# Packing the input tiles of a three-branch attention mixer, and moving the sample queries' selection behind branch B

## The chip, the cores and the metric

The kernel runs on one NeuronCore of a Trainium2 chip. The metric is the time of one execution in microseconds, the median of several runs. The core has TensorE (PE in the profile, its weight loads PEld), VectorE (DVE), ScalarE (ACT), GpSimd (POOL) and SyncE (SP), each with its own instruction stream; they wait for each other by semaphores.

## What is computed

Two layers of a streaming encoder, over 512 prompt tokens and 32 sample tokens (which also see 256 cached ones). Each layer is a half-step FFN, a mixer, and a second half-step FFN. Only the mixer changes:

```python
u = rmsnorm(x, P['mix_pre_gain'][l])
(q_lat, kv_lat, k_r, q_b, k_b, v_b, q_c, k_c, v_c, q_i, k_i, w_i,
 g_a, g_b, g_c) = jnp.split(u @ P['w_in'][l], IN_OFFSETS, axis=-1)
...
# A: latent attention with a rotary key of 32, k_rope = rope(k_r, q_pos)
# B: stick-breaking attention, 8 heads of 64
# C: sparse attention: scores from the indexer, top-k keys, then softmax over those
rel = relu(einsum('bqhd,bkd->bqhk', q_i, k_i) * D_IDX ** -0.5)
score = einsum('bqhk,bqh->bqk', rel, w_i * H_IDX ** -0.5)
_, sel = lax.top_k(score, kk)      # kk = 128 for the prompt, 72 for the sample
...
merged = (sigmoid(g_a) * (o_a @ w_br[0]) + sigmoid(g_b) * (o_b @ w_br[1]) + sigmoid(g_c) * (o_c @ w_br[2]))
x = x + rmsnorm(merged @ w_o, P['mix_post_gain'][l])
```

The widths in u @ w_in: index keys (ki) 64, C's keys (kc) 64, C's values (vc) 64, rotary key (kr) 32, index weights (wi) 8, index queries 512, C's queries 512, latents 384 and 256, B's queries, keys and values 512 each.

## The kernel before

All activations are held feature-major, 128 features on the partitions by 544 tokens. A product of u with 128 columns of weights is a "tile". To keep fp32 accuracy with one-pass matmuls both factors are split into a high and a low part: for each tile ScalarE copies the weights' high half to `piece_m` (`high`, L1118), GpSimd subtracts it in the ring of weights (`low`, L424), and TensorE does 3 x 8 x 2 matmuls of 272 columns (`split_product`, L621 with the high half and L626 with the low one). Products of small factors (`product`, L582) are plain fp32.

The tiles of a mixer have a fixed order, `TILES`. Two PSUM units of two banks each take turns: tile t goes to unit t % 2. TensorE opens a tile when the one before it on the same unit has been evacuated (`vacated`), and the evacuating engine waits for `done`. The order and who evacuates:

- kI (index keys, twice, so that both halves of the partitions hold them), qI0-3, kC (C's keys, twice), vw (C's values and index weights), all by ScalarE, which first makes the high half of the weights two tiles on (`evac`) and then copies. kI and qI0 are computed together (`first_pair`), since u arrives piece by piece. `to_keys` (L1199 to L1201) evacuates with three copies: prompt tokens in two parts, sample tokens.
- v0, v1 (B's values, tokens on the partitions, L734), in four weight pieces that each feed five token blocks; the vw tile is transposed between them.
- The indexer loop: 16 steps of an index score pair (L754), with qC0-3 cut into spans of 12 matmuls between them (L828). VectorE sums the scores over the heads (L1553).
- kr and krs: the rotary key and its half-swapped copy, each four times over on the partitions; then ql0-2, kv0-1, qB0-3, kB0-3. Column sums of squares (L596, two fp32 matmuls of 272 columns against ones) are put between some of them.
- Branch B (L876 to L928) on TensorE, ScalarE and VectorE in a chain, with one round of the top-k search for query block 3 after each of VectorE's steps.
- uq0-3 (evacuated by ScalarE), qr0, qs0, qr1, qs1 (by VectorE, which multiplies with the rotary factors, L1588), kA0-3, vA0-3 (ScalarE). Then attention A and C with the merges (L859) in between, and the output projection wo0-7.

VectorE's order in a mixer: index sums, `select(1)`, `select(2)`, `rotate_keys` (L1662 to L1666), the norms of the latents, `select(4)` (the sample queries: 9 MAX8 and 8 MATCH_REPLACE8 over 288 scores at L1632 and L1634, and eight closing instructions at L1647 to L1654), branch B, `select_last(3)` (the same eight closing instructions over 512 scores), then qr0. GpSimd also issues the DMAs for caches and output rows (`row`), and after branch B splits its output (L498, L500). SyncE loads the weights into a ring of four slots, `MIX_CHUNKS`: the chunk k + 4 is asked for when the last tile that uses chunk k is done.

Of the kernel before, what the change touches and what calls it, by code (L numbers as in the profile page):

```python
# [34 lines left out]
P = 128  # L35
DEPTH, D, D_FF = 2, 1024, 2816
SEQ, NEW, PAST = 512, 32, 256
TOK = SEQ + NEW
# [32 lines left out]
PC_MIX = 30 + 48 + 8  # L71
# [56 lines left out]
IN_PIECES = ([(i // 2, (i % 2) * 1024, 1024) for i in range(6)]  # L128
             + [(3, 0, 1024)] + [(4 + i // 2, (i % 2) * 1024, 1024) for i in range(4)]
             + [(6 + i // 2, (i % 2) * 1024, 1024) for i in range(19)])  # L130
# [3 lines left out]
PIECE_OF = {t: i for i, t in enumerate(TILES[:7])} | {t: 11 + i for i, t in enumerate(TILES[9:28])} | {f"wo{n}": 78 + n for n in range(KD)}  # L134
# [3 lines left out]
def build(nc, d):  # L138

    with ExitStack() as ctx:  # L140
# [15 lines left out]
        cst = sb("cst", [P, 6, P])  # L156
# [61 lines left out]
        kr_raw = region(22296, 2, TOK)  # L218
# [109 lines left out]
        def _(sp):  # L328
# [78 lines left out]
        def _(pool):  # L407
# [27 lines left out]
            for l in range(DEPTH):  # L435
# [33 lines left out]
                evacuated("kI")  # L469
                row("p_ki", kI[0:DH, 0:SEQ], "rows_ki")  # L470
                row("s_ki", kI[0:DH, KEY_NEW:NKEY], "rows_ki")
                lows(4, 13)
                evacuated("v0")
                evacuated("v1")
                evacuated("kC")
# [6 lines left out]
                lows(13, 30)  # L482
# [19 lines left out]
                def gate_low(m):  # L502
                    low(l, PC_M, 30 + 2 * m, (CH_M + 20 + m, 0), 0, 1024)

                def branch_low(m):
                    low(l, PC_M, 31 + 2 * m, (CH_M + 20 + m, 1), 1024, 512)
# [32 lines left out]
                for n, (ch, at, m) in enumerate(OUT_PIECES):  # L539
                    low(l, PC_M, 78 + n, (CH_M + ch, n % 2), at, m)  # L540
# [6 lines left out]
        def _(pe):  # L547
# [144 lines left out]
            def mixer(l):  # L692
# [10 lines left out]
                def split_tile(name, x_h, x_l, chunk_of, at):  # L703
                    t, piece = TILE[name], PIECE_OF[name]
                    open_tile(l, t % 2, T_M + t // 2)
                    split_product(l, t % 2, l * PC_LAYER + PC_M + piece, piece % 2, ring_r[:, (ch + chunk_of) % NSLOT, at:at + 1024],
# [6 lines left out]
                for i in range(2, 7):  # L713
# [11 lines left out]
                for i in range(4):  # L725
                    piece = 7 + i
# [22 lines left out]
                for p in range(16):  # L749
# [6 lines left out]
                    tile_span(l, f"qC{p // 4}", u_h, u_lo, IN_PIECES[11 + p // 4], 12 * (p % 4), 12 * (p % 4) + 12)  # L756
# [12 lines left out]
                for i in range(8):  # L769
                    w = chunk(l, ch + 16 + i // 4)  # L770
                    at = (i % 4) * KQ * P
                    tile(TILES[28 + i], [(w[:, at + k * P:at + k * P + P], ql[:, k, :]) for k in range(KQ)])
# [60 lines left out]
            def merge_span(l, m, u, a, e):  # L833

                b = MERGES[m][0]
                piece = l * PC_LAYER + PC_M + 30 + 2 * m
# [241 lines left out]
        def _(act):  # L1078
# [92 lines left out]
            def mixer(l):  # L1171
                def high_in(i):
                    if i < 30:
                        ch, at, n = IN_PIECES[i]
                        high(CH_M + ch, 0, i % 2, at, n, l)
                    elif 78 <= i < 78 + KD:
                        ch, at, n = OUT_PIECES[i - 78]
                        high(CH_M + ch, 0, i % 2, at, n, l)
# [28 lines left out]
                to_keys("kI", kI)  # L1207
# [14 lines left out]
                high_in(9)  # L1222
# [3 lines left out]
                A(wI[:, 0:4, :], vw[:, :, DH:DH + H], ACT.Copy)  # L1226
                A(VC[:, 6, :], PS[:, 6, 0:DH], ACT.Copy)
                A(wI[:, 4, :], PS[:, 6, DH:DH + H], ACT.Copy)
                for i in range(1, 3):
                    act.wait_ge(S["v_step"], l * 3 + i + 1)  # L1230
                    high_in(9 + i)
                for n in range(2):
                    u = evac(f"v{n}")
                    if n:
                        high_in(12)
# [183 lines left out]
        def _(dve):  # L1419
# [118 lines left out]
            def mixer(l):  # L1538
# [234 lines left out]
def shape_constants():  # L1773
# [3 lines left out]
    cst = np.zeros((P, 6, P), np.float32)  # L1777
# [5 lines left out]
    cst[:, 5] = np.where((k < CHUNK) & (q >= CHUNK), -BIG, 0)  # L1783
    pos = np.concatenate([np.arange(SEQ), PAST + np.arange(NEW)]).astype(np.float32)
# [116 lines left out]
```

## Time and profile before

| | |
|---|---|
| runs, median | 3258.82 us (3257.35 to 3259.65, 3 runs) |
| profiled execution | 3259.87 us |
| its span, first to last instruction | 3258.1 us |
| granted clock of TensorE, mean | 0.982 of 2.4 GHz |
| PE busy | 3078.2 us (94%) |
| PEld busy | 2855.6 us (88%) |
| DVE busy | 1546.2 us (47%) |
| ACT busy | 958.5 us (29%) |
| POOL busy | 1067.7 us (33%) |
| DMA | 255.48 MB, mean 78 GB/s |

### The profile page before, as it was taken

Reading aid. Unit: us, or ns where it says so; the run is one execution under the profiler, and the core shown is the slowest. Engines: PE = TensorE matmul, PEld = TensorE weight load, DVE = VectorE, ACT = ScalarE, POOL = GpSimd, SP = SyncE. Lnnn points to the kernel's source line nnn. Section 1 sums busy time; section 2 is a strip of 40 time slices with the busy share of each in tenths; the row PEclk is TensorE's granted clock in tenths of the full one; section 3 lists DMA queues with packets and bytes.
Section 4 is the critical chain, followed back from the end, with each engine's and each line's share of the span. In section 5 each row is a group of like instructions: output and inputs, shape, how many; then the busy total and the mean of one; then the engine's idle time right before and its main releaser. Section 6 shows DMA issues by size and latency. Waiting matters only on the chain. (4 is left out here: it accounts for less than half of the span.)

```text
span 3258.1 us, 54238 instructions
## 1 busy us (share of the span) xinstructions
PE 3078.2 (94%) x22974; PEld 2855.6 (88%) x22974; DVE 1546.2 (47%) x1857; ACT 958.5 (29%) x1519; POOL 1067.7 (33%) x499
## 2 busy tenths in 40 slices
PE   8999979999999989999899999799999899899997
PEld 7999977956878979999899999679578789899997
DVE  4554242862355446553265532338533554555523
ACT  3222233362333232222232222332623332322221
POOL 3434323312222323343333433333022324244332
PEclk9999989999999999999999999899999999999998
DMA  6221232112111222222212212312021113222221
GB/s 177 86 82 67 88 122 82 69 45 66 41 54 55 89 93 78 90 82 72 105 65 90 86 63 97 123 69 80 21 75 40 62 41 104 85 81 90 78 81 63
DMA packets 43103, 255.48 MB, mean 78 GB/s; under 512 B 6048, under 2 KB 6144, under 8 KB 26048
## 3 DMA queue, kind: packets, MB, share of 16 engines
q1 hardware_dynamic: 37008, 235.64, 20.3%
q0 software_dynamic: 5840, 17.50, 2.0%
q8 instruction: 117, 1.92, 0.2%
q14 instruction: 42, 0.34, 0.0%
q10 hardware_dynamic: 96, 0.08, 0.0%
HBM read 237.34 MB, written 15.85 MB: 78 GB/s over the span
## 5 line engine op out<-in xcount | busy, mean ns | idle before, releaser
L424 POOL TENSOR_TENSOR ring_r<-ring,piece_h 128x1024 fp32r<-128x1024 f32 (+1 forms) x240 | 630.7, 2630 | 1019.3 <-ACT piece_h L1118 1019.3
L424 POOL TENSOR_TENSOR ring_r<-ring,piece_m 128x1024 fp32r<-128x1024 f32 (+1 forms) x172 | 366.5, 2135 | 909.9 <-ACT piece_m L1118 909.7
L1118 ACT ACTIVATE piece_h<-ring 128x1024 fp32r<-128x1024 f32 (+1 forms) x240 | 274.7, 1146 | 1147.4 <-PE PS L626 1138.6
L621 PE MATMUL PS<-uT_r,piece_h 128*128 128x272 f32 x2688 | 555.1, 288 | 6.1 <-DVE sq L1520 6.1
L621 PE MATMUL PS<-u_l,piece_h 128*128 128x272 f32 x2688 | 554.9, 288 | 0.0
L626 PE MATMUL PS<-uT_r,ring_r 128*128 128x272 f32 x3328 | 449.9, 287 | 0.0
L626 PEld LDWEIGHTS PS<-uT_r,ring_r 128*128 128x128 f32 x3328 | 429.6, 188 | 0.0
L621 PEld LDWEIGHTS PS<-uT_r,piece_h 128*128 128x128 f32 x2688 | 421.8, 188 | 7.0 <-ACT piece_h L1118 7.0
L621 PEld LDWEIGHTS PS<-u_l,piece_h 128*128 128x128 f32 x2688 | 419.4, 188 | 0.0
L621 PE MATMUL PS<-act_l,piece_h 128*128 128x272 f32 x1408 | 292.1, 289 | 0.0
L621 PE MATMUL PS<-act_h,piece_h 128*128 128x272 f32 x1408 | 291.5, 288 | 0.0
L1473 DVE TENSOR_TENSOR rstd<-rstd,sq 128x544 f32<-128x544 f32 x36 | 106.7, 2964 | 359.0 <-ACT sq L1090 359.0
L1118 ACT ACTIVATE piece_m<-ring 128x1024 fp32r<-128x1024 f32 (+1 forms) x172 | 160.6, 936 | 340.0 <-PE PS L626 220.0
L1522 DVE TENSOR_TENSOR sq<-sq,rstd 128x544 f32<-128x544 f32 x88 | 219.2, 2491 | 83.8 <-ACT sq L1137 83.8
L621 PEld LDWEIGHTS PS<-act_l,piece_h 128*128 128x128 f32 x1408 | 220.7, 188 | 0.0
L621 PEld LDWEIGHTS PS<-act_h,piece_h 128*128 128x128 f32 x1408 | 220.5, 189 | 0.0
L1530 DVE TENSOR_TENSOR act_l<-sq,act_h 128x544 f32 x88 | 214.0, 2432 | 10.8
L626 PE MATMUL PS<-act_h,ring_r 128*128 128x272 f32 x1408 | 186.5, 287 | 0.0
L626 PEld LDWEIGHTS PS<-act_h,ring_r 128*128 128x128 f32 x1408 | 180.5, 188 | 0.0
L859 PE MATMUL PS<-uT_r,piece_m 128*128 128x272 f32 x768 | 166.6, 299 | 1.9 <-DVE xT L1613 1.9
L859 PE MATMUL PS<-u_lm,piece_m 128*128 128x272 f32 x768 | 161.3, 292 | 0.0
L1527 DVE TENSOR_TENSOR act_h<-sq,PS 128x544 f32 x88 | 63.5, 721 | 168.9 <-PE PS L626 168.3
(248 smaller groups left out, 4715.0 us busy)
## 6 DMA issues: line engine op xcount, KB each, us to landing
ring<-in_w_up SPq DMA_DIRECT2D x88, 1024.0 KB, 4.7
ring<-in_w_dn SPq DMA_DIRECT2D x64, 704.0 KB, 4.1
ring<-in_w_mg SPq DMA_DIRECT2D x48, 768.0 KB, 4.4
ring<-in_w_in SPq DMA_DIRECT2D x24, 1024.0 KB, 4.8
ring<-in_w_out SPq DMA_DIRECT2D x8, 1024.0 KB, 4.8
x_spill<-xT SPq DMA_DIRECT2D x2, 2176.0 KB, 8.9
xT<-x_spill SPq DMA_DIRECT2D x2, 2176.0 KB, 9.1
ring<-in_w_vb SPq DMA_DIRECT2D x4, 1024.0 KB, 4.8
```

The source lines that it names most:

```text
L424: nc.gpsimd.tensor_tensor(ring_r[:, ch[0] % NSLOT, at:at + n], w, hi, ALU.subtract).then_inc(S["w_low"], 1)
L621: mm(PS[:, 2 * u + b, 0:HALF], w, x[k][:, HALF * b:HALF * b + HALF], start=first and k == 0 and n == 0, stop=False)
L626: ins = mm(PS[:, 2 * u + b, 0:HALF], w_l[:, k * P:(k + 1) * P], x_h[k][:, HALF * b:HALF * b + HALF], start=False, stop=last and k == K - 1)
L859: ins = mm(PS[:, 2 * u + j % 2, 0:HALF], w, x[:, k, half], start=j < 2, stop=j >= 6 * K - 2)
L1118: A(buf[:, hs, 0:n], ring[:, ch % NSLOT, at:at + n], ACT.Copy).then_inc(S["w_high"], 1)
L1473: ins = V.tensor_tensor(rstd[:], rstd[:], sq[:, k % 2, :], ALU.add) if k else V.tensor_copy(rstd[:], sq[:, 0, :])
L1522: V.tensor_tensor(g, g, rstd[:], ALU.mult).then_inc(S["gate_step"], 1)
L1527: V.tensor_tensor(halves(hi), halves(g), up, ALU.mult).then_inc(S["gate_step"], 1)
L1530: V.tensor_tensor(lo, g, hi.bitcast(F32), ALU.subtract).then_inc(vacated[1], 1)
```

## The change

The columns of w_in are packed anew. The first tile, "kk", holds the index keys in rows 0 to 63 and C's keys in rows 64 to 127; ScalarE copies each of them to both halves of its destination, in 12 copies of 64 partitions. The tile vw now holds C's values (rows 0 to 63), the rotary key (64 to 95) and the index weights (96 to 103). The tiles kr and krs stay as PSUM tiles, but are made from vw's rows 64 to 95 by a 0/1 matrix in the constants, one plain product of 32 rows each. So the mixer has 27 weight pieces instead of 30, and an empty tile "pad" keeps the count of tiles even. B's value weights come in four chunks of 1024. VectorE does `select(4)` after branch B, behind `select_last(3)`.

```diff
-PC_MIX = 30 + 48 + 8
+N_IN = 27
+PC_MIX = N_IN + 48 + 8
...
-    t = ["kI"] + [f"qI{i}" for i in range(4)] + ["kC", "vw", "v0", "v1"]
+    t = ["kk"] + [f"qI{i}" for i in range(4)] + ["vw", "v0", "v1"]
     t += [f"qC{i}" for i in range(4)] + ["kr", "krs"] + [f"ql{i}" for i in range(KQ)] + [f"kv{i}" for i in range(KKV)]
...
-    t += [f"kA{i}" for i in range(4)] + [f"vA{i}" for i in range(4)]
+    t += [f"kA{i}" for i in range(4)] + [f"vA{i}" for i in range(4)] + ["pad"]
...
+V_CHUNKS = 4
+LATE_TILES = TILES[8:12] + TILES[14:27]
 MIX_CHUNKS = ([("w_in", i, 2048, TILES[2 * i + 1]) for i in range(3)]
-              + [("w_vw", 0, 1024, "vw"), ("w_vb", 0, 2048, "v1"), ("w_vb", 1, 2048, "v1")]
-              + [("w_in", 3 + i, 2048 if i < 9 else 1024, TILES[min(10 + 2 * i, 27)]) for i in range(10)]
+              + [("w_vb", i, 1024, f"V{i}" if i + 1 < V_CHUNKS else "v1") for i in range(V_CHUNKS)]
+              + [("w_in", 3 + i, 2048 if i < 8 else 1024, LATE_TILES[min(2 * i + 1, 16)]) for i in range(9)]
...
-        cst = sb("cst", [P, 6, P])
+        cst = sb("cst", [P, 8, P])
...
-                    if by in TILE:
+                    if by in V_DONE:
+                        sp.wait_ge(S["v_step"], l * 3 + V_DONE[by])
+                    elif by in TILE:
                         consumed(l, TILE[by] % 2, turn_of(by))
...
-                for i in range(2, 7):
+                for i in range(2, 6):
                     split_tile(TILES[i], u_h, u_lo, IN_PIECES[i][0], IN_PIECES[i][1])
...
-                for i in range(15, 30):
-                    name = TILES[9 + i - 11]
-                    split_tile(name, u_h, u_lo, IN_PIECES[i][0], IN_PIECES[i][1])
+                for i, name in enumerate(("kr", "krs")):
+                    tile(name, [(cst[64:96, 6 + i, :], vw_f[64:96, 0:TOK])])
+                for name in LATE_TILES[4:]:
+                    split_tile(name, u_h, u_lo, *IN_PIECES[PIECE_OF[name]][:2])
...
                 for name in ("vA2", "vA3"):
                     pe.wait_ge(vacated[TILE[name] % 2], l * T_LAYER + turn_of(name) + 3)
+                alone(pe)
+                pe.sem_inc(done[TILE["pad"] % 2], 1)
+                pe.sem_inc(vacated[TILE["pad"] % 2], 1)
...
-                to_keys("kI", kI)
+                u = evac("kk")
+                for r, dst in ((0, kI), (DH, kC)):
+                    for e in range(2):
+                        to = dst[DH * e:DH * e + DH]
+                        A(to[:, 0:HALF], PS[r:r + DH, 2 * u, 0:HALF], ACT.Copy)
+                        A(to[:, HALF:SEQ], PS[r:r + DH, 2 * u + 1, 0:SEQ - HALF], ACT.Copy)
+                        ins = A(to[:, KEY_NEW:NKEY], PS[r:r + DH, 2 * u + 1, SEQ - HALF:HALF], ACT.Copy)
+                ins.then_inc(vacated[u], 1)
...
-                to_keys("kC", kC)
                 to_blocks("vw", vw_f)
...
-                select(l, 4, 3)
                 dve.wait_ge(S["rows_ki"], 16 * (l * 2 + 2))
                 branch_b(l)
-                select_last(l, 3, 4)
+                select_last(l, 3, 3)
+                select(l, 4, 4)
                 dve.wait_ge(S["rows_out"], 16 * (l * 12 + 12))
...
+    m = np.arange(P)
+    cst[64 + m % ROPE, 6, m] = 1
+    cst[64 + (m + ROPE // 2) % ROPE, 7, m] = 1
...
-    cols = np.concatenate([part["ki"], part["ki"], part["qi"], part["kc"], part["kc"], part["qc"],
-                           part["kr"], part["kr"], part["kr"], part["kr"], krs, krs, krs, krs, part["ql"], part["kv"],
-                           part["qb"], part["kb"], part["kv"][:128]])
+    none = np.full(P, at[-1])
+    cols = np.concatenate([part["ki"], part["kc"], part["qi"], part["vc"], part["kr"], part["wi"], none[:24],
+                           part["qc"], part["ql"], part["kv"], part["qb"], part["kb"], none])
```

## Rows read from the trace of the kernel before

**Rows 1.** The page's head.
```profile
span 3258.1 us, 54238 instructions
```

**Rows 2.** Windows: length, busy us (instructions) of PE, PEld, DVE, ACT, POOL, clock, DMA, GB/s.
```profile
573.90:669.00 95.10, 94.76 (x741) 93.74 (x739) 75.26 (x161) 27.31 (x48) 36.47 (x18) 1.00 0.23 80
739.95:790.00 50.05, 49.36 (x204) 32.16 (x205) 14.16 (x14) 9.85 (x14) 7.08 (x2) 0.97 0.15 48
```

**Rows 3.** Timeline of ACT, first layer: start, us, engine, line, operation [idle before <- releaser].
```profile
467.35 0.38 ACT L1199 ACTIVATE arena<-PS 128x272 f32<-128x272 f32 x1
...
467.96 1.07 ACT L1118 ACTIVATE piece_m<-ring 128x1024 fp32r<-128x1024 f32 x1
...
573.99 1.06 ACT L1118 ACTIVATE piece_m<-ring 128x1024 fp32r<-128x1024 f32 x1 [0.99 <-PE PS L828]
574.96 0.61 ACT L1205 ACTIVATE arena<-PS 128x544 f32<-128x544 f32 x1
...
580.00 1.06 ACT L1118 ACTIVATE piece_m<-ring 128x1024 fp32r<-128x1024 f32 x1 [4.44 <-PE PS L626]
...
598.01 1.06 ACT L1118 ACTIVATE piece_m<-ring 128x1024 fp32r<-128x1024 f32 x1 [3.92 <-PE PS L626]
...
604.95 1.06 ACT L1118 ACTIVATE piece_m<-ring 128x1024 fp32r<-128x1024 f32 x1 [4.85 <-PE PS L626]
```

**Rows 4.** Timeline of PE, first layer.
```profile
468.13 0.52 PE L621 MATMUL PS<-uT_r,piece_m 128*128 128x272 f32 x2 [1.53 <-ACT arena L1201]
...
500.50 0.47 PE L734 MATMUL PS<-piece_m,uT_r 128*128 128x512 f32 x1 [2.06 <-ACT arena L1214]
...
739.95 4.68 PE L582 MATMUL PS<-arena,ring 128*128 128x272 f32 x12 [0.68 <-ACT arena L1345]
...
746.91 30.26 PE L582 MATMUL PS<-arena,ring 128*128 128x272 f32 x116
```

**Rows 5.** Window of the first weights' arrival, columns as in rows 2.
```profile
12.00:14.00 2.00, 0.00 (x0) 0.00 (x0) 0.00 (x0) 0.98 (x2) 1.07 (x1) 1.00 0.98 410
```

**Rows 6.** Timeline of DVE, first layer.
```profile
648.27 0.45 DVE L1632 MAX8 m<-xT 128x8 f32<-128x288 f32 x1
...
658.34 2.05 DVE L1647 TENSOR_SCALAR xT<-xT,m 128x288 f32<-128x288 f32 x1
...
661.31 0.37 DVE L1650 TENSOR_SCALAR xT<-xT,m 128x288 f32<-128x288 f32 x1
...
664.33 0.55 DVE L1673 MEMSET arena<- 128x256 f32 x2 [0.19 <-DVE arena L1654]
...
672.07 0.42 DVE L1680 SCALAR_TENSOR_TENSOR arena<-PS,sq 128x256 f32<-128x256 f32 x1 [7.19 <-ACT sq L1338]
...
750.07 5.62 DVE L1651 TENSOR_TENSOR_SCAN xT<-xT 128x512 f32<-128x512 f32 x1
...
758.28 0.72 DVE L1588 TENSOR_TENSOR arena<-PS,ropes 128x544 f32<-128x544 f32 x1 [0.39 <-PE PS L582]
...
760.96 0.72 DVE L1588 TENSOR_TENSOR arena<-PS,ropes 128x544 f32<-128x544 f32 x1 [1.96 <-PE PS L582]
```

**Rows 7.** Timeline of DVE, second layer.
```profile
2370.84 0.73 DVE L1588 TENSOR_TENSOR arena<-PS,ropes 128x544 f32<-128x544 f32 x1 [0.40 <-PE PS L582]
```

**Rows 8.** Timeline of POOL, first layer.
```profile
657.82 2.40 POOL L424 TENSOR_TENSOR ring_r<-ring,piece_m 128x1024 fp32r<-128x1024 f32 x1 [3.61 <-ACT piece_m L1118]
...
749.76 4.85 POOL L500 TENSOR_TENSOR o_l<-arena,o_h 128x2176 fp32r<-128x2176 f32 x1
```

**Rows 9.** Windows of 1 us, columns as in rows 2.
```profile
501.00:502.00 1.00, 1.00 (x4) 0.76 (x3) 0.00 (x0) 0.00 (x0) 0.98 (x1) 0.57 1.00 426
532.00:533.00 1.00, 0.00 (x0) 0.00 (x0) 0.00 (x0) 0.99 (x2) 1.00 (x1) 1.00 0.84 319
2765.00:2766.00 1.00, 1.00 (x7) 1.00 (x6) 0.00 (x0) 0.00 (x0) 0.00 (x0) 0.50 1.01 244
```

**Rows 10.** The chain that ended last, in order of time: start, us, what.
```profile
2764.47 5.65 PE PS L621 x32
```

More of the change, by code:

```diff
@@ L126 @@
 assert len(MIX_CHUNKS) == CH_MIX
-IN_PIECES = ([(i // 2, (i % 2) * 1024, 1024) for i in range(6)]
-             + [(3, 0, 1024)] + [(4 + i // 2, (i % 2) * 1024, 1024) for i in range(4)]
-             + [(6 + i // 2, (i % 2) * 1024, 1024) for i in range(19)])
+IN_PIECES = ([(i // 2, (i % 2) * 1024, 1024) for i in range(6)] + [(3 + i, 0, 1024) for i in range(V_CHUNKS)]
+             + [(7 + i // 2, (i % 2) * 1024, 1024) for i in range(17)])
+assert len(IN_PIECES) == N_IN
 OUT_PIECES = [(44 + i // 2, (i % 2) * 1024, 1024) for i in range(KD)]
-PIECE_OF = {t: i for i, t in enumerate(TILES[:7])} | {t: 11 + i for i, t in enumerate(TILES[9:28])} | {f"wo{n}": 78 + n for n in range(KD)}
+PIECE_OF = {t: i for i, t in enumerate(TILES[:6])} | {t: 10 + i for i, t in enumerate(LATE_TILES)} | {f"wo{n}": N_IN + 48 + n for n in range(KD)}
+V_DONE = {f"V{i}": i + 1 for i in range(V_CHUNKS - 1)}
 VA_KEYS = [(0, 1), (2, 3), (4, 5), (6,)]
@@ L468, in _ @@
                 lows(2, 4)
-                evacuated("kI")
+                evacuated("kk")
                 row("p_ki", kI[0:DH, 0:SEQ], "rows_ki")
                 row("s_ki", kI[0:DH, KEY_NEW:NKEY], "rows_ki")
-                lows(4, 13)
+                lows(4, 12)
                 evacuated("v0")
                 evacuated("v1")
-                evacuated("kC")
                 row("p_kc", kC[0:DH, 0:SEQ])
@@ L502, in gate_low @@
                 def gate_low(m):
-                    low(l, PC_M, 30 + 2 * m, (CH_M + 20 + m, 0), 0, 1024)
+                    low(l, PC_M, N_IN + 2 * m, (CH_M + 20 + m, 0), 0, 1024)
                 def branch_low(m):
-                    low(l, PC_M, 31 + 2 * m, (CH_M + 20 + m, 1), 1024, 512)
+                    low(l, PC_M, N_IN + 1 + 2 * m, (CH_M + 20 + m, 1), 1024, 512)
                 pool.wait_ge(S["sb_out"], l * 5 + 5)
@@ L539, in _ @@
                 for n, (ch, at, m) in enumerate(OUT_PIECES):
-                    low(l, PC_M, 78 + n, (CH_M + ch, n % 2), at, m)
+                    low(l, PC_M, N_IN + 48 + n, (CH_M + ch, n % 2), at, m)
                 ffn(l, PC_B, CH_B)
@@ L705, in split_tile @@
                     open_tile(l, t % 2, T_M + t // 2)
-                    split_product(l, t % 2, l * PC_LAYER + PC_M + piece, piece % 2, ring_r[:, (ch + chunk_of) % NSLOT, at:at + 1024],
+                    split_product(l, t % 2, l * PC_LAYER + PC_M + piece, (piece if piece < N_IN else piece - N_IN) % 2, ring_r[:, (ch + chunk_of) % NSLOT, at:at + 1024],
                                   x_h, x_l)
@@ L725, in mixer @@
                 for i in range(4):
-                    piece = 7 + i
+                    piece = 6 + i
                     slot, at, _ = IN_PIECES[piece]
@@ L771, in mixer @@
                     at = (i % 4) * KQ * P
-                    tile(TILES[28 + i], [(w[:, at + k * P:at + k * P + P], ql[:, k, :]) for k in range(KQ)])
+                    tile(TILES[27 + i], [(w[:, at + k * P:at + k * P + P], ql[:, k, :]) for k in range(KQ)])
                     if i == 0:
@@ L835, in merge_span @@
                 b = MERGES[m][0]
-                piece = l * PC_LAYER + PC_M + 30 + 2 * m
+                piece = l * PC_LAYER + PC_M + N_IN + 2 * m
                 w_l = ring_r[:, (CH_M + 20 + m) % NSLOT, :]
@@ L1172, in high_in @@
                 def high_in(i):
-                    if i < 30:
+                    if i < N_IN:
                         ch, at, n = IN_PIECES[i]
                         high(CH_M + ch, 0, i % 2, at, n, l)
-                    elif 78 <= i < 78 + KD:
-                        ch, at, n = OUT_PIECES[i - 78]
-                        high(CH_M + ch, 0, i % 2, at, n, l)
+                    elif N_IN + 48 <= i < N_IN + 48 + KD:
+                        ch, at, n = OUT_PIECES[i - N_IN - 48]
+                        high(CH_M + ch, 0, (i - N_IN) % 2, at, n, l)
                 high_in(0)
@@ L1805 @@
     swap = np.concatenate([np.arange(16, 32), np.arange(16)])
-    krs = part["kr"][swap]
-    cols = np.concatenate([part["ki"], part["ki"], part["qi"], part["kc"], part["kc"], part["qc"],
-                           part["kr"], part["kr"], part["kr"], part["kr"], krs, krs, krs, krs, part["ql"], part["kv"],
-                           part["qb"], part["kb"], part["kv"][:128]])
+    none = np.full(P, at[-1])
+    cols = np.concatenate([part["ki"], part["kc"], part["qi"], part["vc"], part["kr"], part["wi"], none[:24],
+                           part["qc"], part["ql"], part["kv"], part["qb"], part["kb"], none])
     w_in = a["w_in"].reshape(L, KD, P, -1)
+    w_in = np.concatenate([w_in, np.zeros((L, KD, P, 1), np.float32)], axis=3)
     def tiles(w, n):
@@ L1853 @@
         "w_dn": a["w_ffn_down"].reshape(L, 2, 2, 11, P, KD, P).transpose(0, 1, 5, 2, 4, 3, 6).reshape(L, 32, P, 1408),
-        "w_in": groups(tiles(w_in[..., cols], 26), 2),
-        "w_vb": w_in[..., part["vb"]].reshape(L, 2, 4, P, 512).transpose(0, 1, 3, 2, 4).reshape(L, 2, P, 2048),
-        "w_vw": tiles(np.concatenate([w_in[..., vcwi], np.zeros((L, KD, P, P - len(vcwi)), np.float32)], axis=3), 1),
+        "w_in": groups(tiles(w_in[..., cols], 24), 2),
+        "w_vb": w_in[..., part["vb"]].reshape(L, 4, 2, P, 512).transpose(0, 1, 3, 2, 4).reshape(L, 4, P, 1024),
         "w_uq": groups(tiles(uq[..., uq_cols], 8), 4),
```

19 lines of the change are left out of this document (9 added, 10 removed).

## Prediction

> **What bounds the kernel now.** I read the page first, then the stages of the mixer as windows, then the timelines of ScalarE, TensorE, VectorE and GpSimd through one mixer, and last the same places in the second layer. The span is 3258.1 us [rows 1]. The stretch from the last piece of the indexer loop to branch B has TensorE busy for 94.76 of 95.10 us, and the stretch behind branch B for 49.36 of 50.05 us [rows 2]. So in both stretches that the change touches, TensorE sets the pace: an instruction taken from it shortens the kernel by its whole length, and anything that makes it wait lengthens the kernel by the whole wait. The question is how much of either there is, and how much slack VectorE has in each of the two.
>
> **What is removed.** One split tile (a 128-wide output tile of u @ w_in, 48 matmuls of 272 columns) takes 6.0 us: ScalarE starts the high half of the next weights when each tile is done, at 573.99 and then at 580.00 [rows 3]. Three such tiles go from each mixer: the tile of C's keys ahead of the value pieces, and the rotary key and its swapped copy behind the indexer loop. That is 3 x 6.0 = 18.0 us per layer, all of it TensorE's. Their three weight passes on ScalarE and GpSimd go too, beside TensorE, and their DMA is not waited for; they count nothing. Likewise nothing: the value weights in four chunks of 1024 instead of two of 2048 (one chunk is still asked for some three pieces before it is used), the padded vw tile (same 128 columns), and the new order of slots.
>
> **What is added, term by term, per layer.**
> - The packed first tile: nine more copies. Before, its three copies took from 467.35 to 467.96, 0.61 us, and TensorE waited 1.53 us for the last of them before the third tile could open [rows 3, 4]. Now there are four sets of three, each on 64 partitions. If a copy costs by its columns, the extra is 3 x 0.61 = 1.8 us, all in that wait; if half the partitions cost half, the four sets are worth two of the old, and the extra is 0.6 us. Nothing in the trace is cheaper for fewer partitions, so I take 1.8 and keep 0.6 for the range. The rule on ScalarE is the same: the Trainium skill (ScalarE: Activation LUTs, section What ACT_TABLE_LOAD costs) counts an ACTIVATE by elements per lane, 186 ns + 0.833 ns each, with some 93 ns of overlap between neighbours. By it a set would be 0.73 us and the extra 2.2; the row has 0.61, and the sum goes by the row.
> - Rotary key and its swap, now selected from the packed tile by a matrix of ones: 2 fp32 matmuls of 272 columns each. The same pair is seen where a column sum of squares is put between two tiles: 604.95 - 598.01 = 6.94 us instead of 6.01, so 0.93 us a pair [rows 3]. The second must wait for the unit of qC3: its weight pass and copy take from 573.99 to about 575.58 (574.96 + 0.61), 1.6 us. So 1.6 + 0.93 = about 2.6 us until the next tile starts, with 1.9 (both products, no wait) and 3.5 (ScalarE's copy of the first is waited for too) as bounds.
> - The empty tile "pad": one nop and two increments on TensorE, 0.1 us, at most 0.3.
> - Constants of 8 instead of 6 planes: 131 KB more in a start where the queues move 410 GB/s and ScalarE waits for weights [rows 5]: 0.3 us, once; none at the least, 0.6 at the most.
>
> **What is moved.** The selection for the sample queries, select(4), leaves its place before branch B and follows select_last(3) behind it. It issues no DMA. In its old place it ran from 648.27 to 664.33, and VectorE's first job of branch B then still waited 7.19 us for ScalarE [rows 6]: it was hidden, and taking it away frees nothing. It also was no obstacle for the shorter stretch: TensorE now starts branch B 9.4 us earlier after the indexer loop (12.0 - 2.6), and without select(4) VectorE is free at 648.3, over 11 us before that. Had it stayed, its end with the two MEMSETs at 664.9 would have been at most 2 us behind that first job (672.07 - 9.4 = 662.7). Branch B itself is unchanged.
>
> In the new place VectorE has almost no slack. It finished select_last(3) at 757.89, because it had waited only 0.39 us for the product of qr0 when it started on it at 758.28 [rows 6]; in the second layer that wait is 0.40 [rows 7]. Now it first does select(4). Length: 664.33 - 648.27 = 16.06 us as shown, but in it the comparison of L1647 took 2.05 us while GpSimd's weight pass ran from 657.82 to 660.22, and the like comparison at 661.31 took 0.37 [rows 6, 8]. In the new place GpSimd has finished its split (749.76 + 4.85 = 754.6) and waits for weights until attention [rows 8], so I take 16.06 - 1.68 = 14.4 us and keep 16.1 as the upper bound. The Trainium skill gives the reason (GPSIMD Engine Reference, section Specifications: GpSimd shares its SBUF interfaces with VectorE, and the two contend when VectorE reads through both ports); by that rule the lower value holds, and the trace agrees, 2.05 against 0.37 us.
>
> Who waits: qr0 and qs0 are evacuated by VectorE, and the next tile on qr0's unit is qr1. VectorE reaches qr0 at 757.9 + 14.4 = 772.3 and frees it at 773.1 (0.72 us, and a step to signal). TensorE has finished qs0 at 760.9, where VectorE's wait of 1.96 us for it ends [rows 6]. It stands still 773.1 - 760.9 = 12.2, with the signal 12.3 us; bounds 11.5 and 14.0. Behind it in TensorE's queue are qr1, qs1, the eight kA and vA tiles and all of attention, 30.26 us of unbroken matmuls from 746.91 for a start [rows 4]; nothing there waits for something that was not delayed as well, so the stall is not given back.
>
> Then the clock. After the gap before the output projection TensorE ran at the lower of its two levels, 1.2 GHz (granted 0.50 at 2765), and 32 matmuls took 5.65 us instead of the 4.0 that are their share of a 6.0 us tile [rows 9, 10]. In the first layer 12 matmul records behind branch B took 4.68 us, against some 2.7 for such a tile in the run that follows [rows 4]. A stall of 12 us ends the same way: 1.8 us, between 1.6 and 2.2.
>
> Sum per layer: -18.0 + 1.8 + 2.6 + 0.1 + 12.3 + 1.8 = +0.6 us. Twice that, and 0.3 at the start, is +1.5.
>
> One more term is open. The gap before the third tile grows from 1.5 to 3.4 us. A gap of 2.06 us ahead of the value pieces was followed by the lower level (0.57 in the window at 501), while a longer one behind them, in which the window at 532 lies whole, went by at 1.00 [rows 4, 9]. By the price above a fall costs 1.6 us. I count it in one of the two layers, +1.6, with none and both as bounds.
>
> Result: 1.5 + 1.6 = +3.1 us. Made against the profiled execution, 3259.87 us (its span of 3258.1 and 1.8 around it), that is 3263.0; from the median of the runs, 3258.82, it is **3262 us**. Changes under 0.2%, 6.5 us, can't be told from none here.
>
> **The rivals.**
> - *The stall at qr1 is not there, or is mostly absorbed* (faster). Then the 12.3 and the 1.8 go: 3262 - 28.2 = 3233.8 us in full, 3248 with half of it. It decides by VectorE's slack at qr0, which would have to be over 14 us; both layers show 0.4. For it speaks only that a time saved ahead of branch B is certain, while a stall is worked out. Chance 0.13.
> - *The added waits are all at their upper bound* through one cause, ScalarE and the clock: the 3.4 us gap drops the clock in both layers (+1.6), the copy of kr is waited for too (2 x 0.9 us), and the fall after the stall takes 2.2 (2 x 0.4): 3262 + 4.2 = 3266 us; with select(4) still slowed to 16.1 us, 3269.6. It passes the bound to slower from 3265.3. For it: the clock fell after a shorter gap. Against: GpSimd is idle there. Chance 0.26.
> - *The change does not do what it says*: the stretch before branch B does not shorten, because VectorE's chain of selections, not TensorE, starts it. Then 9.4 us of the gain are lost in each layer: 3281 us. Against it are the 7.19 us of slack and the 14 us that VectorE no longer has to do there. Chance 0.03.
> - The forecast, within 3252.3 to 3265.3: 0.58.
>
> **How the numbers follow.** Faster by over 0.2%: the first rival, 0.13. Slower: the second and third, 0.29. The same: 0.58. Bounds of the forecast: all low ends, 2 x (-18.0 + 0.6 + 1.9 + 11.5 + 1.6) = -4.8, give 3254; all high ends give 3270. The range reaches a little into the first rival, to 3251, and ends at 3270; outside it are most of the first rival and the third.
>
> **What would show each step.** In the new trace: per layer 3 x 48 fewer matmuls of the split product before branch B, and 4 fp32 ones with 32 rows; the third tile's wait near 3.4 us; from the indexer loop's end to branch B 85.7 instead of 95.1 us; VectorE at MAX8 of 288 columns directly behind L1654's last step after branch B; a wait of TensorE for VectorE before qr1 of about 12 us, in both layers, with a lower granted clock behind it; the stretch behind branch B near 64 us instead of 50. The prediction is wrong if that wait is under 6 us or over 16, or if the stretches before branch B shorten by other than 13 to 14 us per layer.

## The result, and the profile after

The changed kernel takes **3275.5 us**, the median of five runs (3269.5 to 3277.45), against 3257.6 us for the kernel before in the same comparison. The ratio is 1.0047, with a 95% interval of 1.0033 to 1.0062: slower, by about 18 us. The prediction was 3262 us with a range to 3270, so the time lies outside it, on the slow side. The profiled execution of the changed kernel is one of its fastest, 3269.5 us with a span of 3267.7 us.

The page's head and its row for TensorE:

```profile
span 3267.7 us, 53682 instructions
...
PE 3056.2 (94%) x22702; PEld 2829.2 (87%) x22702; DVE 1537.5 (47%) x1857; ACT 955.5 (29%) x1525; POOL 1051.9 (32%) x493
```

There are 272 matmuls fewer: 288 of the six split tiles are gone, 16 of the four kr and krs products have come. The removal took place, and yet the span grew by 9.6 us. The waits of TensorE, as total us, times, longest one:

```profile
PE PS L587 <- DVE arena L1603: 24.6, 2, 12.3
...
PE PS L626 <- ACT arena L1222: 7.5, 2, 3.7
```

The first is new: the stall ahead of qr1, once in each layer. The second was 3.1 us in all before, 1.53 at the longest. VectorE's timeline shows where it comes from [rows 6 has the same engine before]:

```profile
744.38 0.43 DVE L1669 TENSOR_SCALAR arena<-xT 128x512 bf16<-128x512 f32 x1
744.91 0.46 DVE L1647 MAX8 m<-xT 128x8 f32<-128x288 f32 x1
...
754.99 0.37 DVE L1662 TENSOR_SCALAR xT<-xT,m 128x288 f32<-128x288 f32 x1
...
758.82 0.31 DVE L1669 TENSOR_SCALAR arena<-xT 128x288 bf16<-128x288 f32 x1
759.30 1.36 DVE L1603 TENSOR_TENSOR arena<-PS,ropes 128x544 f32<-128x544 f32 x2 [0.17 <-DVE arena L1669]
```

`select(4)`, the rows on 288 columns, starts at 744.91 right behind `select_last(3)` and ends at 759.13, 14.2 us later; its comparison takes 0.37 us here, not the 2.05 of [rows 6]. Only then are qr0 and qs0 taken out of PSUM, in one go, for both had long been done. TensorE's timeline of the places where the change adds or moves a wait:

```profile
470.32 0.82 PE L626 MATMUL PS<-uT_r,piece_m 128*128 128x272 f32 x2 [3.75 <-ACT arena L1222]
...
498.17 0.47 PE L739 MATMUL PS<-piece_m,uT_r 128*128 128x512 f32 x1 [2.06 <-ACT arena L1230]
...
529.64 0.70 PE L759 MATMUL PS<-arena 64*128 64x256 f32 x4 [3.00 <-ACT arena L1252]
...
569.97 1.18 PE L587 MATMUL PS<-arena,cst 32*128 32x272 f32 x4
571.70 1.27 PE L587 MATMUL PS<-arena,cst 32*128 32x272 f32 x4 [0.55 <-ACT arena L1214]
572.90 0.82 PE L626 MATMUL PS<-uT_r,piece_m 128*128 128x272 f32 x2
...
760.17 6.16 PE L587 MATMUL PS<-arena,ring 128*128 128x272 f32 x18 [12.31 <-DVE arena L1603]
```

And the stretches of [rows 2] as windows (the first now begins with kr and krs, the second with uq0; the third is the second one's like in the second layer), with two short windows inside the first (columns as in rows 2):

```profile
569.97:658.17 88.20, 86.77 (x654) 84.72 (x653) 59.45 (x128) 25.81 (x48) 31.16 (x16) 0.98 0.22 74
728.57:791.64 63.07, 49.70 (x204) 32.25 (x205) 25.77 (x47) 10.21 (x14) 7.08 (x2) 0.89 0.12 39
2345.80:2412.17 66.37, 53.03 (x204) 34.39 (x205) 25.77 (x47) 10.18 (x14) 7.09 (x2) 0.86 0.11 37
...
573.00:576.00 3.00, 3.00 (x13) 3.00 (x14) 2.38 (x9) 0.62 (x1) 0.57 (x1) 0.50 0.38 161
...
578.00:581.00 3.00, 3.00 (x26) 3.00 (x25) 2.17 (x9) 0.36 (x1) 0.00 (x0) 1.00 0.01 3
```

The last two are the same kind of work, split products of 272 columns, with TensorE never idle: 13 matmuls in 3 us at a granted clock of 0.50 (1.2 GHz), 26 at 1.00 (2.4 GHz). What is done at the lower level takes twice as long. Such short stretches turn out to be the subject of this case.

I put one number on them for each kernel, the **low-clock work**: over windows of 1 us from 400 us to the end, the busy time of TensorE times twice what the granted clock lacks to 1.00, added up. It is the time for which TensorE worked at the lower level, and half of it is what the level cost. The kernel before has 61.7 us of it, the changed one 80.9. Half of the difference is 9.6 us, and the spans differ by 9.6 us. So by this count all of the slowdown of this pair of executions is clock, and the rest of the change, stall included, adds up to zero. Experiments 7, 9 and 11 test it.

### The profile page after: what moved, and what is told of

Same layout as the page of the kernel before. It is cut to its first block and busy times, and to the rows that moved or that the text cites. A ratio compares the mean times of both kernels' runs of the same rounds, so it can differ in the third digit from the quotient of the medians.

```text
span 3267.7 us, 53682 instructions
## 1 busy us (share of the span) xinstructions
PE 3056.2 (94%) x22702; PEld 2829.2 (87%) x22702; DVE 1537.5 (47%) x1857; ACT 955.5 (29%) x1525; POOL 1051.9 (32%) x493
## 5 line engine op out<-in xcount | busy, mean ns | idle before, releaser
L430 POOL TENSOR_TENSOR ring_r<-ring,piece_m 128x1024 fp32r<-128x1024 f32 (+1 forms) x166 | 350.9, 2118 | 933.5 <-ACT piece_m L1127 933.3
L631 PE MATMUL PS<-uT_r,ring_r 128*128 128x272 f32 x3232 | 436.8, 287 | 0.0
L631 PEld LDWEIGHTS PS<-uT_r,ring_r 128*128 128x128 f32 x3232 | 417.2, 188 | 0.0
```

The source lines that it names most:

```text
L430: nc.gpsimd.tensor_tensor(ring_r[:, ch[0] % NSLOT, at:at + n], w, hi, ALU.subtract).then_inc(S["w_low"], 1)
L631: ins = mm(PS[:, 2 * u + b, 0:HALF], w_l[:, k * P:(k + 1) * P], x_h[k][:, HALF * b:HALF * b + HALF], start=False, stop=last and k == K - 1)
```

## The experiments

All kernels are the changed one (or the one before, where it says so) with the edit shown. The first four ran beside the kernel before on one chip (3259.04 us there), the next four on one (3259.16), the last four on one (3259.20). All results in one table:

| kernel | median us | ratio to before, 95% interval | profiled span | low-clock work | span less half of it |
|---|---|---|---|---|---|
| before | 3257.6 | | 3258.1 | 61.7 | 3227.3 |
| changed | 3275.5 | 1.0033 to 1.0062 | 3267.7 | 80.9 | 3227.3 |
| 1 select back | 3243.49 | 0.9937 to 0.9962 | 3241.8 | 78.7 | 3202.5 |
| 2 select behind qr | 3244.96 | 0.9943 to 0.9969 | 3242.6 | 80.7 | 3202.3 |
| 3 before, move alone | 3286.41 | 1.0070 to 1.0096 | 3284.6 | 65.7 | 3251.8 |
| 4 stall filled | 3269.78 | 1.0019 to 1.0037 | 3269.5 | 86.7 | 3226.2 |
| 5 = 2 + kk shared | 3228.54 | 0.9896 to 0.9926 | 3225.5 | 50.3 | 3200.4 |
| 6 = 2 + kr early | 3231.90 | 0.9902 to 0.9929 | 3232.7 | 67.3 | 3199.1 |
| 7 all gaps filled | 3252.33 | 0.9972 to 0.9990 | 3250.3 | 41.1 | 3229.8 |
| 8 = 2 + 5 + 6 | 3229.70 | 0.9893 to 0.9923 | 3227.9 | 64.4 | 3195.7 |
| 9 before, gaps filled | 3253.92 | 0.9980 to 0.9998 | 3251.7 | 46.6 | 3228.4 |
| 10 = 8, filled | 3229.42 | 0.9895 to 0.9923 | 3229.3 | 67.2 | 3195.7 |
| 11 = 1, filled | 3230.01 | 0.9896 to 0.9925 | 3229.0 | 50.6 | 3203.7 |
| changed, again | 3275.56 | 1.0030 to 1.0055 | 3273.7 | 92.1 | 3227.7 |

The last column is the kernel's time with the clock's share taken out. It falls into groups that follow the waits alone, as the experiments show one by one.

**The moved selection (1, 2, 3).** Number 1 puts `select(4)` back, number 2 puts it later still, number 3 does the move alone to the kernel before.

```diff
 # 1
+                select(l, 4, 3)
                 dve.wait_ge(S["rows_ki"], 16 * (l * 2 + 2))
                 branch_b(l)
-                select_last(l, 3, 3)
-                select(l, 4, 4)
+                select_last(l, 3, 4)
 # 2
                 select_last(l, 3, 3)
-                select(l, 4, 4)
...
                     dve.wait_ge(S["qr_ready"], l * 2 + g + 1)
+                select(l, 4, 4)
                 attend(l, 0)
```

> The changed kernel with select(4) put back ahead of branch B; all of the packing stays. Theory A (the move costs TensorE 12.3 us of waiting per layer ahead of qr1, and 2 to 3 us of lower clock behind it): about 2 x 15 = 30 us below the changed kernel's 3275, so 3245, and 12 us below the kernel before. Rival B (the packing is what costs, through its own gaps and the lower clock that they leave, and the move is mostly covered): less than 10 us below the changed kernel, 3265 or more. VectorE should reach branch B in time; if it is late, by 2 us per layer at most.

> The changed kernel with select(4) moved further back, behind the two rotary query tiles (qr, qs) and ahead of attention, where VectorE was seen idle for 23 us. Theory A: the wait ahead of qr1 is gone and 14.4 us fit into the idle time, so the same as with select(4) ahead of branch B, about 3245. Rival (VectorE's work anywhere behind branch B delays attention): the start of attention is late by 5 us or more per layer, 3255 or more.

> The kernel before with only select(4) moved behind select_last(3); nothing of the packing. Theory A: 12.3 us of waiting and 2 to 3 us of lower clock per layer more than before, 3258 + 29 = 3287. Rival B: under 10 us more, below 3268. If the two parts add up, the distance of this kernel from the one before and that of the changed kernel from the one with select(4) put back are alike within 4 us.

The move alone costs 27.4 us (3286.41 against 3259.04). Its waits show the two stalls and nothing else of that size:

```profile
PE PS L582 <- DVE arena L1588: 24.6, 2, 12.3
```

With the clock taken out, the move is worth 3251.8 - 3227.3 = 24.5 us, which is the wait. Undoing it in the changed kernel gives 3202.5, which is 24.8 lower. In the medians the two differ more: 27.4 us in the kernel before, 32.0 in the changed one (3275.5 and 3243.49), where alike within 4 us had been expected. The rest is the clock: half of the low-clock work is 2.0 us more with the move in the kernel before, and 6.7 more in the changed one by its repeated run (92.1 and 78.7). Behind the qr and qs tiles it costs nothing either, since VectorE is then waited for by no tile; TensorE's run through that place, in number 2, has no gap:

```profile
743.68 25.12 PE L587 MATMUL PS<-arena,ring 128*128 128x272 f32 x94
768.63 1.88 PE L794 MATMUL PS<-ring,arena 128*128 128x512 f32 x4
```

So without the move the change is a gain of some 15 us (0.4 to 0.6%), and the stall is of the size that was predicted.

**The clock behind the stall (4).** 25 products of no use for TensorE ahead of qr1, so that the wait stays but TensorE works in it.

```diff
+                    if i == 6:
+                        filler(25)
```

> The changed kernel with 25 fp32 matmuls of 272 columns of no use, 11.3 us, put on TensorE ahead of qr1, where it otherwise waits 12.3 us for VectorE; they write a free bank. Theory C (the low clock behind the wait costs 1.8 us in the first layer and 2.6 in the second): 4.4 us less than the changed kernel, near 3271, with the granted clock at 1.00 behind the wait. Rival (the wait alone is the cost, the clock behind it costs nothing): no difference within 1 us. If the filling delays qr1, it is up to 2 us more.

```profile
743.80 8.41 PE L587 MATMUL PS<-arena,ring 128*128 128x272 f32 x36
752.05 11.62 PE L724 MATMUL PS<-ropes,cst 128*128 128x272 f32 x50
764.44 1.87 PE L587 MATMUL PS<-arena,ring 128*128 128x272 f32 x7 [0.77 <-DVE arena L1610]
```

The window behind it, at 762 to 766, was granted 1.00 (0.52 in the changed kernel at 760 to 764, behind its stall), in both layers. The median fell by some 5.7 us, more than the 4.4 that the two stretches held. But the runs of number 4 go from 3256.15 to 3274.43 us, so that a step of this size says little by itself, and the profiled execution had 86.7 us of low-clock work, more than the changed kernel's 80.9: stretches that its first profile did not have stood at other gaps. One execution was not enough to tell which of them belong to the kernel.

**The changed kernel again.** For that reason the same kernel was run once more.

> The changed kernel once more, unchanged, to see which of its low-clock stretches a second profiled execution has. Theory 1 (the stretches differ between executions, as its times of 3269.5 to 3277.5 us do): a profile with another set of them, and a span that differs by half of the difference in work done at the low clock. Rival: the same stretches and the same span, 3267.7 us.

This execution, 3275.46 us, is the one at the median. Two windows of it beside the same two of the first profile, first the repeated run:

```profile
500.00:503.00 3.00, 2.80 (x7) 2.25 (x8) 0.00 (x0) 0.00 (x0) 1.67 (x1) 0.52 0.29 113
534.00:537.00 3.00, 3.00 (x14) 2.74 (x16) 0.84 (x2) 0.60 (x2) 2.99 (x6) 0.55 0.75 246
```

and the first profile of the changed kernel:

```profile
500.00:503.00 3.00, 3.00 (x15) 2.44 (x14) 0.00 (x0) 0.00 (x0) 0.00 (x0) 1.00 0.00 0
534.00:537.00 3.00, 3.00 (x23) 2.31 (x22) 1.17 (x3) 0.66 (x2) 0.00 (x0) 1.00 0.61 199
```

The waits ahead of both are the same to 0.01 us in the two executions, 2.06 and 3.00 us; one lost the clock behind them and the other did not. The low-clock work is 92.1 against 80.9 us, half of the difference is 5.6, and the spans differ by 6.0 us. Its six runs go from 3263.39 to 3277.74 us. Against the kernel before it is (92.1 - 61.7) / 2 = 15.2 us of 15.6.

**All gaps filled, in both kernels (7, 9).** If the clock is the whole loss, the two kernels must come out alike once TensorE is hardly still in these gaps. Number 7 also keeps the 25 products of number 4 ahead of qr1.

```diff
 # 7 (9: three ahead of the third tile, four, six)
+                filler(8)
                 for i in range(2, 6):
                     split_tile(TILES[i], u_h, u_lo, IN_PIECES[i][0], IN_PIECES[i][1])
...
+                filler(4)
                 banks = [2 * (TILE[f"v{s // 2}"] % 2) + s % 2 for s in range(4)] + [4]
...
+                filler(6)
                 pe.wait_ge(S["cache_in"], (l * N_CACHE + N_CACHE) * 16)
...
                 for i, name in enumerate(("kr", "krs")):
+                    if i:
+                        filler(1, 5)
```

> The changed kernel with additional products of no use in each of the gaps that it has on TensorE ahead of branch B and ahead of the qr tile (8 ahead of the third tile, 4 ahead of the v tiles, 6 behind them, 1 between kr and krs, 25 ahead of the rotated query), so that the waits stay and TensorE is never still in them. Theory 1 (the low-clock stretches are what is left of the loss): all stretches of both layers go, 10 to 17 us less than the changed kernel, 3258 to 3265 us. Rival (the stretches come anyway, at another place): no better than with the filling at the rotated query alone, 3268 to 3272 us.

> The kernel before with additional products of no use in its own three gaps (3 ahead of the third tile of the mixer's inputs, 4 ahead of the v tiles, 6 behind them), so that its waits stay and TensorE isn't still in them. Theory (a low-clock stretch follows each of these gaps and costs half of the work done in it): the stretches of before that lie there go, 5 to 10 us less, 3249 to 3254 us, so that the two kernels come out alike once their gaps are filled (3252 us with the change). Rival (the fillings helped the changed kernel for another reason): no change, 3259 us.

Filling took 23 us from the changed kernel, more than either theory had said, since I had worked from its first, fortunate profile; half of 92.1 - 41.1 would be 25.5. The kernel before gained 5.3 us; half of its 61.7 - 46.6 would be 7.6. The products themselves cost 1 to 2.5 us where they outlast the wait, as the table's last column shows (3229.8 and 3228.4 against 3227.3). Filled, the two stand at 3252.3 and 3253.9 us: the difference of 18 us is gone, although qr1 of number 7 still comes only when VectorE has freed its unit. The same windows behind the gap ahead of the v tiles, first of the kernel before and then of it with its gaps filled:

```profile
500.00:504.00 4.00, 3.50 (x10) 2.77 (x11) 0.00 (x0) 0.24 (x2) 1.98 (x1) 0.64 0.55 233
```
```profile
500.00:504.00 4.00, 3.77 (x17) 2.83 (x16) 0.00 (x0) 0.58 (x3) 2.31 (x1) 1.00 0.54 229
```

Numbers 9 and 7, in this order, also give the terms of the change at an even clock, first layer: from the pair of the first two tiles to the third tile 15.92 and 18.36 us, third tile to v 32.37 and 26.35, indexer loop's end to branch B 95.59 and 86.66, uq0 to attention 48.39 and 61.22.

**The select back, filled (11).** The fillings of number 7 in number 1.

> The changed kernel with the select moved back ahead of branch B and additional products in the gaps (8, 4, 6 and 1). Theory: the clock is that of the changed kernel with all gaps filled (3252 us), and the two stalls of 12.3 us are gone, 3228 us; against the filled kernel before (3249 to 3254 us) that is the worth of the packing without its waits' clock, 21 to 26 us. Rival: 3232 to 3240 us, the filling does less here.

3230.0 us, 23.9 below the filled kernel before: this is the worth of the packing with its stall and its clock taken away, 12 us a layer. The rival of 3232 to 3240 is excluded by the run's own spread (3229.15 to 3230.80).

**Shorter waits instead of fillings (5, 6, 8, 10).** Number 5 lets VectorE copy C's keys while ScalarE copies the index keys; number 6 puts the kr and krs products behind the v tiles, into the 3.00 us gap; number 8 does both, and number 10 fills what gaps it has left. All have the select where number 2 has it.

```diff
 # 5, ScalarE and VectorE
-                for r, dst in ((0, kI), (DH, kC)):
-                    for e in range(2):
+                for e in range(2):
+                    to = kI[DH * e:DH * e + DH]
+                    A(to[:, 0:HALF], PS[0:DH, 2 * u, 0:HALF], ACT.Copy)
...
+                for e in range(2):
+                    to = kC[DH * e:DH * e + DH]
+                    V.tensor_copy(to[:, 0:HALF], PS[DH:P, 0, 0:HALF])
...
+                ins.then_inc(S["kk_half"], 1)
 # 6, TensorE, moved up from behind the indexer's loop
+                for i, name in enumerate(("kr", "krs")):
+                    tile(name, [(cst[64:96, 6 + i, :], vw_f[64:96, 0:TOK])])
                 pe.wait_ge(S["cache_in"], (l * N_CACHE + N_CACHE) * 16)
```

> The select behind the qr and qs tiles, as in the second experiment (3245.0 us), and the sets of copies out of the kk tile shared: ScalarE copies the index keys, VectorE C's keys, so that a set should last about 0.37 us on ScalarE instead of 0.74 us, and the third tile of the mixer's inputs should wait about 2.2 us instead of 3.75 us. Theory 1 (only the waits count): 1.5 us less in each layer, 3242 us. Theory 2 (waits and the clock after them): where the shorter gap leaves the clock up, 1.7 us more for each layer, 3238.5 us. Rival: VectorE takes longer for its two copies out of PSUM than ScalarE saves, and the gap stays; 3245 us.

> The select behind the qr and qs tiles, and the kr and krs products of both layers moved ahead of the indexer's loop, right behind the v tiles, where TensorE stood still for 3.0 us. Theory 1 (only the waits count): the kr and krs products fill that gap and their own waits go, 1.4 us less in each layer, 3242 us. Theory 2 (with the clock): the low-clock stretch behind kr and krs (1.7 us a layer) goes too, and that behind the gap ahead of the indexer's loop, 3238.5 us. Rival: the copies of kr and krs on the other engines hold up the first score tiles of the indexer by as much; 3245 us.

> The select behind the qr and qs tiles, the copies out of the kk tile shared between ScalarE and VectorE, and the kr and krs products ahead of the indexer's loop, all three together. Theory 1 (waits alone add up): 3245 less 3 and 3, 3239 us. Theory 2 (with the clock): 3232 to 3236 us. Rival (low-clock stretches only move to other places): 3241 to 3245 us.

> The version with the select behind the qr and qs tiles, shared kk copies and early kr and krs, and additional products in its three gaps (4, 4 and 3). Its profile at 3230 us had 64 us of TensorE work in low-clock stretches, the changed kernel with all gaps filled 41. Theory: half of the difference goes, 12 us, 3218 us. Rival (stretches move to other places whatever is filled): 3227 to 3231 us.

In number 5 the third tile waits 2.29 us instead of 3.75:

```profile
470.15 0.48 PE L627 MATMUL PS<-uT_r,piece_m 128*128 128x272 f32 x2 [2.29 <-ACT arena L1223]
```

The kernel gained 16.4 us on number 2 by the medians, where 0 to 6.5 had been expected, and 17.1 by the profiled spans. Of these, 1.9 us stay with the clock taken out; the other 15.2 are the low-clock work, down from 80.7 to 50.3 us. The stretch behind the third tile, for one, is gone in this execution. First number 2, then number 5:

```profile
471.00:475.00 4.00, 3.04 (x15) 3.04 (x16) 0.00 (x0) 2.78 (x9) 2.41 (x2) 0.68 0.01 3
```
```profile
470.00:474.00 4.00, 3.85 (x31) 3.88 (x32) 0.00 (x0) 1.82 (x5) 3.93 (x3) 1.00 0.16 62
```

So is its like in the second layer. But those behind the v gap (499 to 504 in number 2), the indexer's gap (both layers) and branch B's end (second layer) are gone too, which number 5 did not touch: their waits are as long as ever. The one behind kr and krs stayed, in both layers; here is the first:

```profile
571.00:574.00 3.00, 3.00 (x14) 2.92 (x14) 2.48 (x8) 0.62 (x1) 0.85 (x1) 0.51 0.47 197
```

Number 6 also gained much more than its waits (13.1 us, 3.2 of them with the clock taken out). Number 8 has the shortest time of all with the clock taken out, 3195.7, as the two edits add up (1.9 + 3.2 = 5.1, and 6.6 came), and its median is below all that had been expected for it. But it has 64.4 us of low-clock work and so is no better than number 5. Filling its gaps (10) did nothing: 3229.42 us, the time that the rival named. Its mechanism is not what the traces show, though: the stretches did not move, all but one of them lie where number 8 has its own. Two of the three filled gaps, ahead of the third tile and of v, had no fall behind them in number 8, so there was nothing to win; behind the third, ahead of kr, the fall stayed in both layers. TensorE's timeline of number 10 at this third place, and the window behind it with the clock:

```profile
525.41 1.54 PE L712 MATMUL PS<-ropes,cst 128*128 128x272 f32 x6
526.87 1.18 PE L588 MATMUL PS<-arena,cst 32*128 32x272 f32 x4
528.37 1.18 PE L588 MATMUL PS<-arena,cst 32*128 32x272 f32 x4 [0.32 <-ACT arena L1261]
529.48 0.70 PE L771 MATMUL PS<-arena 64*128 64x256 f32 x4
```
```profile
531.00:534.00 3.00, 3.00 (x13) 2.10 (x12) 0.52 (x2) 0.16 (x1) 1.29 (x3) 0.50 1.00 365
```

TensorE was busy but for 0.32 us, and fell to the lower level all the same. Most of what ran just before were products on 32 and 64 rows; whether that is the reason was not tested. In number 11, where filling stands in this place and kr and krs don't, the window from 531 to 534 has a granted clock of 1.00.

Numbers 5, 8, 10 and 11 lie within 1.5 us of each other, all about 0.9% faster than the kernel before. Number 5 is the simplest that needs no useless products.

## Why the prediction was wrong

Its step "Then the clock", with the open term behind it, failed: it priced a fall of the clock about right and counted too few of them. It allowed for one fall of the clock behind each stall (1.8 us a layer) and one, in one of two layers, for the longer gap at the third tile (1.6 us): 5.2 us. The clock took 9.6 us in the first profile and 15.2 in the one at the median. The low-clock work of the two executions, first and second layer, at the three waits that the change adds or lengthens:

| behind | first profile | repeated run | half of it, both layers | predicted |
|---|---|---|---|---|
| third tile's wait, 3.75 us | 3.2, 3.3 | 3.3, 3.3 | 3.3 | 1.6 |
| kr and krs, with 0.55 us between | 3.4, 3.4 | 3.4, 3.4 | 3.4 | 0 |
| stall, 12.31 us | 3.6, 5.2 | 4.5, 5.2 | 4.4, 4.9 | 3.6 |

That is 11.1 and 11.6 us for the places of the change. The rest of the difference, -1.5 us in one execution and +3.6 in the other, lies at waits that both kernels have, as the v gap at 500, the indexer's at 534 and branch B's end. The stall of the second layer also cost more than its upper bound, 2.6 us against 2.2.

For the open term, the third tile's gap, one layer of two was too few. All six profiled executions in which that wait is 3.75 us (changed, changed again, 1, 2, 4, 6) have the fall in both layers; the four in which it is 1.53 or 2.3 us (before, 3, 5, 8) have it in neither. Behind kr and krs, with their 0.55 us between, the fall came in both layers of all six that have them there unfilled (changed, changed again, 1, 2, 4, 5). The other steps, per layer:

- **Stall at qr1**: predicted 12.3 us, measured 12.31. Length of `select(4)` in its new place: 14.4 predicted, 14.2 measured.
- **Three split tiles less**: predicted -18.0. The one ahead of the v tiles gave -6.02 (9 against 7). The other two and the kr and krs products gave -8.93 at an even clock, where -12.0 + 2.6 = -9.4 was predicted. In the changed kernel itself the stretch is 88.13 us where 85.7 was predicted, most of the difference being the low stretch at 572 to 576. From kr's start to the next tile it is 2.93 us, where 2.6 was predicted.
- **The stretches before branch B**: the prediction called itself wrong if they shortened by other than 13 to 14 us. From the first pair of tiles to branch B they shortened by 11.45 us in the first layer (452.35 to 669.54 before, 452.43 to 658.17 after) and 8.63 in the second (2066.55 to 2283.79, 2066.40 to 2275.01), by 12.4 in the filled pair, first layer. So by its own sign it was wrong here; the other, a wait ahead of qr1 under 6 or over 16 us, did not come.
- **Copies of the kk tile**: predicted +1.8, measured 3.75 - 1.53 = +2.2. A set of three copies of 64 partitions took 0.71 to 0.75 us from start to start, not the 0.61 of the old set. The estimate that the prediction worked out from the figures of the Trainium skill (ScalarE: Activation LUTs, section What ACT_TABLE_LOAD costs) was 0.73 and 2.2, and the trace agrees with it. The old set's 0.61 went from its first start to the start of the weight pass, which overlapped the last copy; to the end of that copy it is 0.73 as well. ScalarE's timeline, second set:

```profile
468.04 0.39 ACT L1220 ACTIVATE arena<-PS 64x272 f32<-64x272 f32 x1
468.34 0.35 ACT L1221 ACTIVATE arena<-PS 64x240 f32<-64x240 f32 x1
468.59 0.18 ACT L1222 ACTIVATE arena<-PS 64x32 f32<-64x32 f32 x1
468.78 0.39 ACT L1220 ACTIVATE arena<-PS 64x272 f32<-64x272 f32 x1
```

- **Sum without the clock**: predicted 2 x -1.2 + 0.3 = -2.1 us, measured 0.0 and +0.4 (last column of the table). This part of the forecast was low by 2.1 to 2.5 us in all, by terms that are each within half a microsecond a layer.

So of the 12.5 us by which the execution at the median lies above the forecast for a profiled one (3275.46 against 3263.0), 10.0 are falls of the clock that I had not counted, and 2.5 the other terms. In the first profile they are 4.4 and 2.1. What I had in hand would have warned me: the row at 501 showed a fall behind a gap of 2.06 us [rows 9], and the change adds or lengthens a wait at three places a layer. I counted the third tile's gap in one layer instead of both, and none behind kr and krs. My other row, the window at 532 at 1.00, lies inside its gap, and the falls seen here come behind a short gap; it could not have shown one. That the clock stayed up behind it too (1.00 at 533 to 538 before) was true of that execution and not of others. I had also read one execution as if its low stretches were the kernel's own. Of the rivals, the second had the right mechanism (3266 us, falls in both layers) and still had none behind kr and krs. It also had the copy of kr waited for; the gap there was 0.55 us. The first (no stall) and the third (no shorter stretch ahead of branch B) are excluded by the wait of 12.3 us and the stretch of 88.1 us.

What stays open is what decides whether a gap is followed by a fall. It isn't the length alone: 2.06 and 3.00 us did both in two executions of one kernel, and over all ten profiled executions with the v gap of 2.06 us unfilled, 8 of 20 were followed by a fall. Why shortening one wait by 1.5 us in number 5 also cleared stretches that lie at waits it did not touch was not separated from the shift of all later work that came with it.

## What to carry to other kernels

Before moving work to an engine with "free" time, find the first tile of another engine that it will stand ahead of there: `select(4)` cost nothing in its old place or behind the qr and qs tiles, and 25 us in between. Where TensorE is the bound, count every gap of a few microseconds twice, by its length and by the stretch at the lower clock that may follow it. Add up the low-clock work of more than one profiled execution before explaining a difference of half a per cent; with it taken out, spans compare to about a microsecond. And useless products in waits that can't be removed are cheap, but what they bring depends on whether a fall follows there: 23 us for the changed kernel, 5 for the one before, nothing for number 8.

## What the runs showed of the hardware

- Spans less half of the low-clock work agree within 0.4 us for the kernel before and two executions of the changed one (3227.3, 3227.3, 3227.7), while the spans themselves differ by up to 15.6 us.
- The granted clock fell behind a short gap, not in it. At 470 us in the changed kernel it was 1.00 in the idle microsecond, and low from then to 474, with TensorE back at work:

```profile
469.00:470.00 1.00, 0.00 (x0) 0.00 (x0) 0.00 (x0) 0.99 (x5) 0.84 (x1) 1.00 0.36 143
470.00:471.00 1.00, 0.68 (x3) 0.68 (x4) 0.00 (x0) 0.98 (x3) 0.00 (x0) 0.63 0.00 0
471.00:472.00 1.00, 1.00 (x6) 1.00 (x6) 0.00 (x0) 0.98 (x4) 0.57 (x1) 0.50 0.00 0
...
474.00:475.00 1.00, 1.00 (x10) 1.00 (x9) 0.00 (x0) 0.00 (x0) 0.84 (x2) 1.00 0.21 49
```

- It also fell with a gap of only 0.32 us, behind products on 32 and 64 rows (number 10, granted 0.50 at 531 to 534, TensorE busy for all of it).
- In the long stall it fell while TensorE stood still: TensorE had stopped at 747.86, and the clock reads 0.58 at 750 to 751 and then 0.50:

```profile
752.00:760.00 8.00, 0.00 (x0) 0.00 (x0) 6.52 (x17) 0.00 (x0) 0.00 (x0) 0.50 0.00 0
760.00:764.00 4.00, 3.83 (x9) 2.98 (x10) 1.38 (x3) 0.00 (x0) 0.00 (x0) 0.52 0.01 4
```

- A TensorE that fills a stall of 12 us with products keeps 1.00 through it and behind it (numbers 4 and 7); one that stands still there comes back at the lower level (granted 0.50 until 763, with the products starting again at 760.17).
- ScalarE's copies out of PSUM took as long on 64 partitions as on 128: 0.37 to 0.39, 0.35 and 0.18 us for 272, 240 and 32 columns, against 0.38, 0.36 and 0.20.
